# Two stages whose x is turned before it is scaled, a Fourier transform split by token parity, and units of weights moved among the steps of the delta rule

## The reference

```python
h = rms_norm(x, even_norm); z = h @ even_w_in           # 2048 -> 7168
x = x + concat(conv branch, attention branch) @ even_w_out
h = rms_norm(x, odd_norm);  z = h @ odd_w_in            # 2048 -> 512 + 256 + 64 + 16 + 2048
cq, ckv, ik, iw, gate = split(z)
x = x + (attention over 64 keys picked by a top-k of index scores * silu(gate)) @ odd_w_out
x = rms_norm(x, final_norm)
h = rms_norm(x, g_mix); q, k, v, z, f, scal, gates = split(h @ w_in)        # 2048 -> 9248
y_a = (gated delta rule, forward and backward, 8 heads of 128, chunks of 64) @ w_dn_up
y_f = real(fft2(f.reshape(256, 8, 128), axes=(tokens, features))) @ w_fourier
x = x + (sigmoid(gates_a) * y_a + sigmoid(gates_f) * y_f) @ w_o
h = rms_norm(x, g_mlp)
x = x + square(relu(h @ w_mlp_up)) @ w_mlp_down         # 2048 -> 8192 -> 2048
out = rms_norm(x, g_final)
```

## Time and profile before

| | before |
|---|---|
| time, median of 3 runs | 2259.07 us (2258.32 to 2259.59) |
| the profiled execution: time / span | 2259.39 us / 2257.6 us |
| mean granted TensorE clock | 0.991 |
| busy TensorE, its weight loads | 2192.3 us (97%), 1882.7 us (83%) |
| busy VectorE, ScalarE | 1026.1 us (45%), 1036.1 us (46%) |
| busy GpSimd | 1717.2 us (76%) |
| HBM read, mean rate of all DMAs | 380.24 MB, 170 GB/s |

### The profile page before, as it was taken

How to read it: one execution, slowest core, us unless ns; L and a number is a source line. 1 busy time by engine, 2 the same in 40 slices (tenths; PEclk the granted TensorE clock), 3 DMA queues, 4 the chain that set the end, 5 groups by cost and what they waited for, 6 DMA issues and landing times.

```text
span 2257.6 us, 34155 instructions
## 1 busy us (share of the span) xinstructions
PE 2192.3 (97%) x12554; PEld 1882.7 (83%) x12554; DVE 1026.1 (45%) x1762; ACT 1036.1 (46%) x1442; POOL 1717.2 (76%) x721
## 2 busy tenths in 40 slices
PE   7999999999999999999999999999999999999997
PEld 6888888878888778888888888887888888888886
DVE  3981242024853141657474834305813822831841
ACT  5434455454556554535354545444333333333343
POOL 6888868877667865657575757897888888888885
PEclk9999999999999999999999999999999999999999
DMA  7666545646455754545454545665666666666664
GB/s 216 189 188 191 181 140 172 193 129 180 140 150 166 228 152 124 146 116 160 116 153 121 159 121 169 204 201 157 190 191 193 187 195 189 192 189 194 187 194 140
DMA packets 321438, 384.10 MB, mean 170 GB/s; under 512 B 14654, under 2 KB 255141, under 8 KB 321061
## 3 DMA queue, kind: packets, MB, share of 16 engines
q1 hardware_dynamic: 317237, 376.75, 55.8%
q10 hardware_dynamic: 4080, 5.64, 0.8%
HBM read 380.24 MB, written 2.10 MB: 169 GB/s over the span
## 4 chain that ended last, share of the span: by engine, by line
PE 92%; DVE 2%; ACT 2%; issue 2%; POOL 1%; DMA 1%; ACTq 0%; POOLq 0%; DVEq 0%
PE lin_ps L1942 36%; PE lin_ps L1945 18%; PE lin_ps L1982 9%; PE lin_ps L1983 9%; PE lin_ps L1981 9%; POOL w_lo L582 1%; PE ps L1914 1%; PE ps L2312 1%; ACT w_hi L610 1%; DMA raw<-in_odd_w_out 0%; PE ps L2244 0%; PE lin_ps L2106 0%; PE lin_ps L2107 0%; PE lin_ps L2108 0%; PE lin_ps L2167 0%
## 5 line engine op out<-in xcount | busy, mean ns | idle before, releaser
L582 POOL TENSOR_TENSOR w_lo<-raw,w_hi 128x1024 fp32r<-128x1024 f32 x716 | 1716.9, 2405 | 521.1 <-ACT w_hi L610 424.2
L1942 PE MATMUL lin_ps<-a,w_hi 128*128 128x512 f32 x3200 | 1022.1, 401 | 0.9 <-POOL w_lo L582 0.8
L610 ACT ACTIVATE w_hi<-raw 128x1024 fp32r<-128x1024 f32 x456 | 479.2, 1059 | 570.1 <-PE lin_ps L1945 359.6
L1945 PEld LDWEIGHTS lin_ps<-a,w_lo 128*128 128x128 f32 x3200 | 602.5, 188 | 142.4
L1945 PE MATMUL lin_ps<-a,w_lo 128*128 128x256 f32 x3200 | 630.4, 278 | 0.0
L1942 PEld LDWEIGHTS lin_ps<-a,w_hi 128*128 128x128 f32 x3200 | 492.3, 190 | 8.6 <-issue 5.2
L621 ACT ACTIVATE w_hi<-raw 128x1024 fp32r<-128x1024 f32 x228 | 242.1, 1062 | 384.8 <-PE lin_ps L1945 225.6
L1981 PE MATMUL lin_ps<-w_hi,b 128*128 128x512 f32 x704 | 274.7, 390 | 1.9 <-POOL w_lo L582 1.8
L1982 PE MATMUL lin_ps<-w_lo,b 128*128 128x512 f32 x704 | 274.0, 389 | 0.0
L1983 PE MATMUL lin_ps<-w_hi,b 128*128 128x512 f32 x704 | 273.9, 389 | 0.0
L1981 PEld LDWEIGHTS lin_ps<-w_hi,b 128*128 128x128 f32 x704 | 132.2, 188 | 30.6 <-POOL w_lo L582 3.3
(11 more groups left out here) (379 smaller groups left out, 2094.0 us busy)
## 6 DMA issues: line engine op xcount, KB each, us to landing
raw<-in_w_in SPq DMA_DIRECT2D x144, 512.0 KB, 3.7
raw<-in_w_mlp_up SPq DMA_DIRECT2D x128, 512.0 KB, 3.8
raw<-in_w_mlp_down SPq DMA_DIRECT2D x128, 512.0 KB, 3.7
raw<-in_even_w_in SPq DMA_DIRECT2D x112, 512.0 KB, 3.7
raw<-in_odd_w_in SPq DMA_DIRECT2D x40, 512.0 KB, 3.7
raw<-in_even_w_out SPq DMA_DIRECT2D x32, 512.0 KB, 3.9
raw<-in_odd_w_out SPq DMA_DIRECT2D x32, 512.0 KB, 4.6
raw<-in_w_o SPq DMA_DIRECT2D x32, 512.0 KB, 4.3
```

Source lines behind the costliest of these rows:

```text
L582: nc.gpsimd.tensor_tensor(w_lo[:, slot], raw[:, slot], w_hi[:, slot].bitcast(F32), ALU.subtract).then_inc(lo_done, 1)
L610: nc.scalar.activation(w_hi[:, slot], raw[:, slot], ACT.Copy).then_inc(hi_done, 1)
L1942: nc.tensor.matmul(lin_ps[:, 2 * parity + m, :], hi[:, k, m * P:(m + 1) * P], src[:, kk].rearrange("p s n -> p (s n)"), start=(q == 0 and ...
L1945: last = nc.tensor.matmul(lin_ps[:, 2 * parity + m, 0:T], lo[:, k, m * P:(m + 1) * P], src[:, kk, 0, :], start=False, stop=(q == n - 1 and ...
```

## The change

- **x unscaled, places 1 and 3** (`LATE`): `projected` turns each block of x as soon as it is added (`turn_x`, after unit 6 of the next block), and the last one after four chunks of the next stage (`turned_in`). `upper` and `lower` follow in ScalarE's and VectorE's order of the projection. The factor 1/rms of a token is applied later (`own_scale`, `by_row`): in the odd layer in the reads of cq, kv and the index key, and for the gates by a multiplication of the drained banks with `by_row`, the factors spread along the free axis by two small matmuls and a ScalarE copy; in the MLP as the square r2 in the addition after the down projection. `a` and `b` swap roles there.
- **Fourier by token parity**: the first transform reads tokens q, q+2, ...; the second then takes 128 columns per parity instead of 256, VectorE forms sum and difference, and ScalarE copies one of them first. Its tables are loaded in five DMAs instead of one.
- **Units ahead of the levels**: in TensorE's order a unit stands ahead of each of levels 4, 5 and 6 (before: one ahead of level 4 alone), and one unit fewer ahead of the first turn of a pair (`to_tokens`) and of the last (`outputs_turned`); ScalarE's casts are moved to match.
- **Sigmoids**: three quarters of each are taken during pair 3, between casts, the rest after the first group of the mixing.

```diff
+LATE = {1: "even_w_out", 3: "w_o_2"}
+SCALED = {0: 0, 2: 1}
+TURN_AT = 6
...
-        r1 = nst[:, 36:38]
+        r1, r2 = nst[:, 36:38], nst[:, 40:42]
+        def late(r, c):
+            return a[:, (c + 8) % DC] if r == 1 else b[:, c]
...
+                def upper(n):
+                    for j in range(4):
+                        c = 4 * n + j
+                        act.wait_ge(nm_pe.sem, nm_pe.at(f"{c // 2}", r))
+                        g = ROWS[NORMS[r]] + c
+                        nc.scalar.activation(late(r, c)[:, 0, :], ps[:, 2 * (n % 2) + j // 2, (j % 2) * T:(j % 2 + 1) * T], ACT.Copy,
+                                             scale=vec[:, g:g + 1]).then_inc(nm_hi.sem, 1)
...
-                for j in range(4, 35):
+                last_turn = 4 if r == 3 else 5
+                for j in range(4, 40):
                     hi(u0 + j, (u0 + j) % SLOTS)
                     if j in (12, 20, 28):
                         added(name, (j - 12) // 8)
                         squares(r, (j - 12) // 8)
-                added(name, NB - 1)
-                squares(r, NB - 1)
+                    if j in (8 + TURN_AT + 3, 16 + TURN_AT + 3, 24 + TURN_AT + 3):
+                        upper((j - TURN_AT - 3) // 8 - 1)
+                    if j == 35:
+                        added(name, NB - 1)
+                        squares(r, NB - 1)
+                    if j == 32 + last_turn:
+                        upper(NB - 1)
                 roots_of(r)
...
+            act.wait_ge(gt_pe.sem, gt_pe.at("rows"))
+            nc.scalar.activation(by_row[:], ps[:, 3, 0:T], ACT.Copy).then_inc(gt_act.sem, 1)
...
-                    act.dma_start(z[:, Z_DFT:Z_DFT + 5, :], t["c_dft"]).then_inc(table_in, 16)
+                    act.dma_start(z[:, Z_DFT, :], t["c_dft"][:, 0, :]).then_inc(table_in, 16)
+                    for q in range(TT):
+                        for k in range(TT):
+                            act.dma_start(z[64 * k:64 * k + 64, Z_DFT + 1:Z_DFT + 3, q * P:(q + 1) * P],
+                                          t["c_dft"][q:P:2, 1 + k:4 + k:2, 0:P]).then_inc(table_in, 16)
...
                 act.wait_ge(fo_pe.sem, fo_pe.at("o", g))
-                nc.scalar.activation(b[:, 8 + g, 0, :], ps[:, 3, 0:T], ACT.Copy).then_inc(fo_act.sem, 1)
+                nc.scalar.activation(z[:, Z_DFT + 3, 0:P], ps[:, 3, P:2 * P], ACT.Copy).then_inc(fo_act.sem, 1)
+                act.wait_ge(fo_dve.sem, fo_dve.at("diff", g))
+                nc.scalar.activation(b[:, 8 + g, 0, :], ps[:, 3, T:2 * T], ACT.Copy).then_inc(fo_act.sem, 1)
...
                 nc.scalar.activation(dz, dz, ACT.Silu).then_inc(dz_act.sem, 1)
-                fill(5, 6)
+                fill(5)
                 silus(other)
+                fill(6)
+                norms(one_way)
                 fill(7)
-                norms(one_way)
+                norms(other)
                 fill(8)
-                norms(other)
+                feats(one_way)
                 fill(9)
-                feats(one_way)
-                fill(10, 11)
                 feats(other)
                 decays(one_way)
+                fill(10, 11)
+                decays(other)
                 fill(12)
-                decays(other)
-                fill(13)
                 keep_m(one_way)
-                fill(14, 15)
+                fill(13, 14)
                 keep_m(other)
-                fill(16, 17, 18, 19, 20, 21)
+                for n in range(15, 21):
+                    fill(n)
+                    if p == PAIRS - 1 and n < 19:
+                        act.wait_ge(group_free, FILL_G + 24)
+                        gate = z[:, 8 * (n - 15):8 * (n - 15) + 6, :]
+                        nc.scalar.activation(gate, gate, ACT.Sigmoid).then_inc(mx_act.sem, 1)
                 turned(one_way)
-                fill(22)
+                fill(21)
                 turned(other)
-                fill(23)
                 for l in (4, 5, 6):
                     for w in ways:
                         level(w, f"x{l}")
-                fill(24)
+                    fill(18 + l)
...
+            mixed(0)
+            act.wait_ge(group_free, GROUP0["gates"] + 16)
+            gate = z[:, 0:32, :].rearrange("p (n r) c -> p n (r c)", n=4)[:, :, 6 * T:8 * T]
+            nc.scalar.activation(gate, gate, ACT.Sigmoid).then_inc(mx_act.sem, 1)
+            with act.Fori(1, 8) as i:
+                mixed(i)
...
+                def lower(n):
+                    for j in range(4):
+                        c = 4 * n + j
+                        dve.wait_ge(nm_hi.sem, nm_hi.at(f"{c | 1}", r))
+                        g = ROWS[NORMS[r]] + c
+                        to = late(r, c)
+                        nc.vector.scalar_tensor_tensor(out=to[:, 1, :], in0=ps[:, 2 * (n % 2) + j // 2, (j % 2) * T:(j % 2 + 1) * T],
+                                                       scalar=vec[:, g:g + 1], in1=to[:, 0, :].bitcast(F32),
+                                                       op0=ALU.mult, op1=ALU.subtract).then_inc(nm_lo.sem, 1)
...
                     for q in range(TT):
-                        xs = x[:, q, _block(n)]
-                        nc.vector.scalar_tensor_tensor(out=xs, in0=xs, scalar=scale[:, q:q + 1] if scale is not None else 1.0,
-                                                       in1=lin_ps[:, 2 * ((g0 + n) % 2) + q, :], op0=ALU.mult,
+                        xs, acc = x[:, q, _block(n)], lin_ps[:, 2 * ((g0 + n) % 2) + q, :]
+                        by = own_scale if own_scale is not None else scale
+                        nc.vector.scalar_tensor_tensor(out=xs, in0=xs if own_scale is None else acc, scalar=by[:, q:q + 1] if by is not None else 1.0,
+                                                       in1=acc if own_scale is None else xs, op0=ALU.mult,
                                                        op1=ALU.add).then_inc(group_free if q else x_half, 1)
-            def to_x_gains(name, rnd, r, before_last):
+                    if r is not None:
+                        lower(n)
+                if r is not None:
+                    for q in range(TT):
+                        reciprocals(r, q)
...
             def gate_out(n):
                 dve.wait_ge(unit_used, OU[f"gate{n}"] + 4)
+                dve.wait_ge(gt_act.sem, gt_act.at("rows"))
+                bank = 2 * (OG[f"gate{n}"] % 2)
+                both = lin_ps[:, bank:bank + 2, :].rearrange("p m (s n) -> p m s n", s=2)
+                nc.vector.tensor_tensor(both, both, by_row[:].unsqueeze(1).unsqueeze(1).broadcast_to([P, 2, 2, T]), ALU.mult).then_inc(gt_dve.sem, 1)
+                dve.wait_ge(gt_dve.sem, gt_dve.at(f"g{n}"))
                 group_out(f"gate{n}", 0, z[:, Z_OGATE + 2 * n:Z_OGATE + 2 * n + 2, :])
...
+            nc.vector.tensor_tensor(stat[:, 50:52], recip, recip, ALU.mult).then_inc(own, 1)
...
+            nc.vector.tensor_tensor(stat[:, 42:44], stat[:, 42:44], recip, ALU.mult).then_inc(own, 1)
...
             for g in range(FG):
+                dve.wait_ge(fo_act.sem, fo_act.at("odd", g))
+                for n, op in ((0, ALU.add), (1, ALU.subtract)):
+                    nc.vector.tensor_tensor(ps[:, 3, T + n * P:T + (n + 1) * P], ps[:, 3, 0:P], z[:, Z_DFT + 3, 0:P], op).then_inc(fo_dve.sem, 1)
                 dve.wait_ge(fo_act.sem, fo_act.at("hi", g))
-                nc.vector.tensor_tensor(b[:, 8 + g, 1, :], ps[:, 3, 0:T], b[:, 8 + g, 0, :].bitcast(F32), ALU.subtract).then_inc(fo_dve.sem, 1)
+                nc.vector.tensor_tensor(b[:, 8 + g, 1, :], ps[:, 3, T:2 * T], b[:, 8 + g, 0, :].bitcast(F32), ALU.subtract).then_inc(fo_dve.sem, 1)
...
+            dve.wait_ge(dn_dve[1].sem, dn_dve[1].at("lo", PAIRS - 1))
+            with dve.Fori(0, 3) as i:
+                mixed(i)
+            dve.wait_ge(mx_act.sem, mx_act.at("late"))
+            mixed(3)
             dve.wait_ge(mg_rs.sem, mg_rs.at("r1"))
             to_x("w_o_2", 3, scale=r1)
-            norm(3)
+            dve.wait_ge(nm_rs.sem, nm_rs.at("rn1", 3))
+            nc.vector.tensor_tensor(r2, recip, recip, ALU.mult).then_inc(sq_dve.sem, 1)
...
+            def turn_x(r, n):
+                name = LATE[r]
+                pe.wait_ge(x_half, NB * PLAIN.index(name) + n + 1)
+                pe.wait_ge(group_free, OUTS[name][1] + n + 1)
+                for half in range(2):
+                    if n >= 2:
+                        pe.wait_ge(nm_lo.sem, nm_lo.at(f"{4 * (n - 2) + 2 * half + 1}", r))
+                    for j in (2 * half, 2 * half + 1):
+                        for q in range(TT):
+                            m = nc.tensor.transpose(ps[:, 2 * (n % 2) + half, (j % 2) * T + q * P:(j % 2) * T + (q + 1) * P],
+                                                    x[:, q, n * BLK + j * P:n * BLK + (j + 1) * P], ident[:])
+                    m.then_inc(nm_pe.sem, 1)
+            def turned_in(r):
+                def wait(c):
+                    if c == 4:
```

(35 more changed lines are left out.)

116 lines of the change are left out of this document (57 added, 59 removed).

## The result

The changed kernel takes 2241.46 us, the median of 4 runs (2240.70 to 2241.67), beside 2258.7 for the kernel before on the same chip: a ratio of 0.9924, 95% interval 0.9907 to 0.9942, faster by 17.2 us. The forecast was 2234, its range 2225 to 2245. The profiled execution took 2241.67 us with a span of 2239.9, 17.7 us less than the one of before, and a mean granted clock of 0.997 (0.991 before). So the time lies inside the whole range, but outside the forecast's own 2230 to 2239.

The account below looks back on a forecast made before the run. TensorE's stream of matrix products was taken to set the time. Terms -6.4 - 6.3 - 6.7 - 15.1 + 6.1 + 6.8 + 0.5 - 3.8 = -24.9 us gave 2234; range 2225 to 2245, the forecast's own 2230 to 2239.

Parts of the forecast that it names:

- rival e: Whole kernel: the weights bind, GpSimd cannot catch up, so all 25 us come back, 2259; chance 0.04.
- rival d: Levels: a unit ahead gives nothing if its weights are not cast; 42 us at 12 levels, 2276; chance 0.03.
- Turnings, Fourier, mixing: Turning x unscaled at two places, -6.4 and -6.3 us; second Fourier transform, -6.7; sigmoids moved from the mixing's start, -3.8.
- rival c: Both turnings: ScalarE's and VectorE's halves of each block hold up casts or chunks, some 3 us, 2240; chance 0.13.
- Gates: Odd layer: one more VectorE pass of 1.23 us for each of eight gates, +6.8 us, bounds 3 and 10.
- Rival (a): Gate passes hidden by slack in TensorE, pair starts too: half of +12.9 us falls away, 2228; chance 0.14.
- Key/value chain: Two added products of tiny vectors: 2.9 us against 2.4 to spare, +0.5 us, bounds 0 and 2.9.
- both at half: Key/value chain: each of the two added products counted at half of the 2.4 us seen in one row.
- Levels: Four pairs: a unit ahead of levels 5 and 6 covers VectorE's updates, -2.5 us a pair, -10.0 in all.
- Clock: Levels of the pairs: three falls of the clock, 1.7 us each, no longer happen, -5.1 us.
- Rival (b): New waits pull the clock down, 1.7 us at the odd gates and each pair start, +8.5, 2243; chance 0.18.
- Pair starts: One unit fewer ahead of first turns: pair 0 waits 1.4 and 1.1 us, pairs 1 to 3 1.2 each, +6.1.

Follow-up runs that it names:

- e7: Changed kernel without the multiplication of the odd layer's gates by each token's factor (gates not normalised, no kernel to use); one execution, 2232.95 us.
- e3: Kernel before with only the new order of units in the four pairs (TensorE's order, ScalarE's casts to match); 2256.35 us, ratio 0.9983.
- e4: Kernel before with only the Fourier branch by token parity and its copies, sums and five table DMAs; 2253.31 us, ratio 0.9972.
- e6: Changed kernel with Fourier branch, order in the pairs and sigmoids put back, leaving x turned unscaled at both places; 2251.59 us, ratio 0.9971.
- e1: Changed kernel with VectorE's two 64-column copies that reset the inverse issued after both convolutions instead of ahead; 2232.13 us, ratio 0.9874.
- e5: Changed kernel with the two resets in place but made by an operation reading one operand from PSUM; 2232.59 us, ratio 0.9888.
- e2: Changed kernel with each odd-layer gate drained first and multiplied afterwards in SBUF, 512 columns instead of 1024 in PSUM; 2241.07 us.
- e8: Version of e1 with gates 2, 3 and 4 drained first and multiplied in SBUF as in e2; 2230.61 us, ratio 0.9875.

## Why the forecast was right, and where it was not

**Bound.** TensorE's stream sets the time throughout. What was won ahead was not waited for behind (rival e): TensorE's waits for GpSimd's lower halves are 3.3 us in all, 5.9 before. No cast holds up a level (rival d: the levels wait for nothing but 0.2 to 0.4 us of ScalarE's copies).

**Turnings, Fourier, mixing.** -6.4, -6.2, -6.7 and -4.0 against -6.4, -6.3, -6.7 and -3.8. ScalarE's and VectorE's halves of each block are hidden (rival c falls), and no sigmoid blocks a cast. The stepped read of weights costs nothing: 8.4 us for 32 instructions in both kernels; the 60 ns of the forecast's bound are in no run. The Trainium skill's rule on 16-byte lines (SBUF — State Buffer, Door 1: The DMA port swizzle), which the forecast named, would allow this, and the trace agrees.

**Gates.** +6.8 forecast and measured, and e7 returns it. Rival (a) falls: there was no slack. The parts were 2.7 after the top-k, 1.3 behind gate 4 and 2.8 in the last rounds, against 3.1, 1.2 and 2.5, so that the sum is exact is chance.

**Key/value chain.** +0.7 against +0.5, but not by the forecast's "both at half": one of the two added products (L1465, two columns) took 2.02 us and ended at 511.46 beside GpSimd's instruction at 511.42, the other (L1472), with GpSimd idle, took 0.16. The sum came out since one late product is two half late ones.

**Levels.** -9.0 instead of -10.0. From the first product of level 4 to the end of the first solve pair 2 of the kernel before takes 12.86 us at full clock, the changed one 16.17, which is 10.60 without the 5.57 us of its two added units. The waits fell by 2.4 us a pair as forecast (3.56 to 1.12), but each of the two further changes from products to small matmuls and back costs some 0.1 us (0.20 us beyond its 16 products for such a unit, 0.09 for others), which the forecast left out.

**Clock.** -4.2 instead of -5.1. The three falls cost 1.2, 1.6 and 1.4 us in pairs 0, 1 and 3, not 1.7 each: the one of pair 0 covers the small products of the first solve, which took 1.73 us at the low clock against 1.26 at the full one in pair 2, less than double. That the falls go with the waits inside the levels is shown by e3. Rival (b) falls: waits of 1.4 to 1.8 us, each by itself, brought no fall.

**Pair starts.** The term that was mis-sized is "Sum 1.4 + 1.1 + 3 x 1.2 = +6.1": it measured +11.1, outside its bounds of 3 and 8. Its reading of the covers (the units of other weights between two steps) was good for pair 0 (2.5 forecast, 2.8 measured), but for pairs 1 to 3 it took VectorE's chain to be as long as before. The chain was 1.5 us longer, since the moved casts changed when GpSimd works, and two copies took 3.34 us instead of 1.82; e3, which has that move and nothing else, shows the same 3.34, and e4 and e6, which do not have it, the 1.82. So 1.2 us each became 2.75. e1 and e5 remove the hold in two ways, and the waits of pairs 1 to 3 are gone in both.

**The sum.** 2241.5 is inside 2225 to 2245 only by the room that was left for rivals (b), 2243, and (c), 2240. Neither took place, so that the time lies beside theirs is chance.

**Open.** The first products come 0.8 us later, and 0.7 us are won at the tables (in e4 as well). Neither can be put down to the change by these traces. The first products come 0.5 to 1.8 us later than in the kernel before in e3, e4 and e6, which change nothing there. From the tables to the third layer e1, e2, e5, e7 and e8, with the same table loads as the changed kernel, differ from it by -2.0 to +0.8 us.

## What to carry to other kernels

When work is moved, look for short copies between SBUF operands on VectorE ahead of a long chain, and see what GpSimd does beside them: their price can be that of GpSimd's instruction (here up to 2.44 us), not their own (0.18). It changes with the timing of GpSimd, so a duration read in the kernel before need not hold in the new order. Move them behind the chain, or use an operation with one operand in PSUM. And take a unit of cover from where the engine that is waited for has time to spare in the new order; that engine may itself be waiting for the units.

## What the runs showed of the hardware

A VectorE copy of 64 columns from SBUF to SBUF took 0.18 to 0.20 us, or 0.90, 1.64 and 2.44 when an instruction of GpSimd of 2.4 us ran, and then ended within 0.06 us of it; as an operation with one operand in PSUM it took 0.21 to 0.23 at the same place. A multiplication of 512 columns in SBUF took 0.69 us with GpSimd idle and 1.72 to 2.95 beside it, one of two columns 0.16 or 2.02. Three waits of TensorE with 2.15 us of idle time in the trace gave back 2.77 us when e1 removed them, so each cost some 0.2 us more than the idle time shown. Thirty-two weight loads with a step of two elements took 8.4 us with their products, as without a step.
